# A two-layer decoder trunk on one core: q, k and z projected transposed, with high and low activations side by side

## The chip, the cores and the metric

The kernel runs on one core of a Trainium2 chip. The metric is the device time of one execution in microseconds (us). The program is written instruction by instruction for each engine: TensorE (PE in the profile; its weight loads are PEld), VectorE (DVE), ScalarE (ACT), GpSimd (POOL) and SyncE (SP, which issues DMAs). Semaphores alone order the engines against each other.

## The reference

The input is 256 tokens of width 2048 in fp32. Layer 0 is retention, layer 1 is sparse attention, each behind an RMS norm and with a SiLU gate. Cut to what matters here:

```python
h = x
hn = rmsnorm(h, norm_g[0])                      # layer 0: retention, 8 heads
q, k, v, gate = split(hn @ ret_w_in)            # per head 256, 256, 512, 512 columns
scores = einsum(q, k * dk**-0.5) * decay
o = groupnorm(scores @ v (+ state))             # per head and token, no gain
h = h + (silu(gate) * o) @ ret_w_out
hn = rmsnorm(h, norm_g[1])                      # layer 1: 16 heads in 4 groups
q, kc, vc, ks, vs, kw, vw, g, z = split(hn @ nsa_w_in)   # 2048, 6 x 512, 48, 2048 columns
k_cmp, v_cmp = mlp(blocks of kc), mlp(blocks of vc)
o = g0*attend(q, k_cmp, v_cmp) + g1*attend(q, ks, vs) + g2*attend(q, kw, vw)   # g = sigmoid
h = h + (silu(z) * o) @ nsa_w_out
out = rmsnorm(h, final_g)
```

## The kernel before

**Weights.** All weights come in chunks of 512 rows by 512 columns (four tiles of 128 rows, 1 MB), 200 in all, through a ring of four slots. SP loads a chunk into `w_raw` when VectorE is through with the chunk four places earlier. ScalarE rounds it to `w_hi` (L417) when TensorE is through with the chunk four places earlier, and VectorE takes the rest, `w_lo = w_raw - w_hi` (L639). Both run two chunks ahead of TensorE (`ahead`). The activations, transposed, are kept in two rounded parts as well, `hT_hi` and `hT_lo`.

**One chunk on TensorE** (`chunk`, L943 to L945). For each of two token tiles and each of four row tiles three products of 512 columns are made, 24 in all; the activations are the stationary operand and the weights stream:

```python
pe.matmul(o, xT_hi[:, k0 + i, tok], w_hi[:, s, i, :], start=a, stop=False)
pe.matmul(o, xT_hi[:, k0 + i, tok], w_lo[:, s, i, :], start=False, stop=False)
ins = pe.matmul(o, xT_lo[:, k0 + i, tok], w_hi[:, s, i, :], start=False, stop=z)
```

A projection of the norm's output takes four such chunks (2048 rows) and ends in a pair of PSUM banks, one for each token tile; an output chunk (`out_chunk`) is complete in itself. There are two pairs of banks in `acc` that take turns, and four `side` banks. A pair is given back as a whole, by `acc_free`.

**From tokens to transposed.** q and k of a head (one projection of 256 + 256 columns), kc, vc, ks, kw, a group's q and a group's z are all needed with features on partitions. VectorE (`take`, L672) or ScalarE (`take_z`, L577, with SiLU) scales the pair by rstd into `stage`, TensorE turns `stage` with eight transposes into `side[0:2]` (L980), and ScalarE and VectorE copy them to qT and kT (L476, L730), rawT, ksT, kwT (L545), qhT (L514) or silu_zT (L583).

**Order of work.** It is written out by hand, as chunks c with steps between them.

- *Retention, head h*: chunks 0 to 3 are q and k, 4 to 7 v, 8 to 11 the gate, 12 to 15 the output of head h - 1 (none for head 0). After chunk 4 the transposes, after chunk 5 the scores (L1016, L1018), after chunk 8 the weighted values (L1026 to L1028), after chunk 0 of the next head the transposes of y. Four more output chunks follow the last head, with the norm's transposes between them.
- *The k/v part*: seven projections (kc, vc, ks, vs, q of group 0, kw, vw), c = 0 to 27. Between them stand the compressions (L1107), the gates (48 products of 256 columns, L1132 to L1134) and the first scores. POOL computes rstd (L368).
- *Groups g = 0 to 3*: group 0 has 8 chunks (z, q of the next group), groups 1 and 2 have 12 (z, q, output of the group before), group 3 has 8 (z, output). The table `SLOTS` says behind which chunk a head's scores (L1081), the transposes of its probabilities (L1153) and the weighted values (L1166, between the two tiles of chunk 7 or 8) come. Each head's scores pass from TensorE to VectorE (add the distances, maximum; `head_scores`), to ScalarE (exponentials; `head_exps`) and to VectorE (`head_probs`, L802 to L810). In VectorE's program `head_probs` stands ahead of the low pass of its chunk (`ahead`), and reads of PSUM stand behind it. Four last output chunks follow group 3.

`add_residual` (L664) adds an output chunk's pair to the residual.

## Time and profile before

| | us |
|---|---|
| median of 3 runs (1268.44 to 1268.94) | 1268.67 |
| the profiled execution's own time | 1269.46 |
| its span, first to last instruction | 1267.7 |
| PE busy | 1244.6 (98%) |
| PEld busy | 1022.0 (81%) |
| DVE busy | 697.7 (55%) |
| ACT busy | 543.8 (43%) |
| POOL busy | 59.3 (5%) |

The span leaves 1.8 us of the profiled execution outside. The mean granted TensorE clock is 0.996 of full speed. The DMA engines moved 221.62 MB at a mean of 175 GB/s. The records of products overlap each other: a 512-column product is on record for 390 to 395 ns and the next one starts before it ends, so a product's cost is the distance from its start to the next start, not its duration. "Idle before" in a row is the time in which the engine had no record open, so a gap between starts is longer by what the last product would have taken anyway.

### The profile page before, as it was taken

The numbers are of one execution on the slowest core, as the hardware profiler recorded it, in microseconds if no ns is written. First come the engines' busy times: TensorE is split into PE (matmuls) and PEld (weight loads), VectorE is DVE, ScalarE is ACT, GpSimd is POOL, SyncE is SP. The second block draws the span as 40 slices with busy tenths as digits, with TensorE's granted clock in tenths as the row PEclk, the third lists the DMA queues.
The fourth block names the chain that finished last, engine by engine and source line by source line (L and its number), as shares of the span: only waits on it lengthen the run. The fifth ranks groups of instructions, "written<-read, shape, count | busy, mean of one in ns | idle before, by whom it ended". The sixth has DMA issues, their size and how long they took to land.

```text
span 1267.7 us, 15041 instructions
## 1 busy us (share of the span) xinstructions
PE 1244.6 (98%) x5734; PEld 1022.0 (81%) x5734; DVE 697.7 (55%) x768; ACT 543.8 (43%) x680; POOL 59.3 (5%) x53
## 2 busy tenths in 40 slices
PE   7999999999999999999999999999999999999997
PEld 6878888888888888888888888888878687887875
DVE  5545465364474564464465576444446475665765
ACT  6344243343342353343334354233346374472653
POOL 1010100100100100100100111000000000000000
PEclk9999999999999999999999999999999999999999
DMA  9635655556455465564564585646434234534432
GB/s 334 240 133 200 199 166 176 188 165 207 157 191 206 146 208 175 165 219 145 165 232 150 163 267 200 201 133 232 166 107 160 100 133 166 166 133 139 159 104 96
DMA packets 129304, 221.62 MB, mean 175 GB/s; under 512 B 6769, under 2 KB 39745, under 8 KB 129009
## 3 DMA queue, kind: packets, MB, share of 16 engines
q1 hardware_dynamic: 127360, 213.94, 50.6%
q0 software_dynamic: 1712, 7.07, 1.8%
q8 instruction: 26, 0.43, 0.1%
q14 instruction: 14, 0.11, 0.0%
q10 hardware_dynamic: 192, 0.08, 0.0%
HBM read 218.96 MB, written 2.10 MB: 174 GB/s over the span
## 4 chain that ended last, share of the span: by engine, by line
PE 98%; DVE 1%; DMA 0%; ACT 0%; issue 0%; POOL 0%; POOLq 0%; DVEq 0%; ACTq 0%
PE acc L943 28%; PE acc L945 28%; PE acc L944 28%; PE side L980 2%; PE side L1081 2%; PE side L1166 2%; PE side L1107 1%; PE side L944 1%; PE side L945 1%; PE side L943 1%; PE side L1153 1%; PE side L1168 1%; PE side L972 1%; PE side L1016 1%; PE side L1028 0%; PE side L1027 0%
## 5 line engine op out<-in xcount | busy, mean ns | idle before, releaser
L639 DVE TENSOR_TENSOR w_lo<-w_raw,w_hi 128x2048 fp32r<-128x2048 f32 x199 | 452.6, 2286 | 219.4 <-ACT w_hi L417 217.3
L943 PE MATMUL acc<-w_hi,hT_hi 128*128 128x512 f32 x1280 | 506.2, 395 | 3.3 <-DVE vw L672 1.5
L945 PE MATMUL acc<-w_hi,hT_lo 128*128 128x512 f32 x1280 | 499.5, 390 | 0.0
L944 PE MATMUL acc<-w_lo,hT_hi 128*128 128x512 f32 x1280 | 498.9, 390 | 0.0
L417 ACT CAST w_hi<-w_raw 128x2048 fp32r<-128x2048 f32 x199 | 374.4, 1909 | 116.0 <-PE acc L945 115.0
L943 PEld LDWEIGHTS acc<-w_hi,hT_hi 128*128 128x128 f32 x1280 | 240.9, 188 | 54.0 <-issue 3.4
L945 PEld LDWEIGHTS acc<-w_hi,hT_lo 128*128 128x128 f32 x1280 | 240.6, 188 | 50.8
L944 PEld LDWEIGHTS acc<-w_lo,hT_hi 128*128 128x128 f32 x1280 | 241.1, 188 | 48.9
L943 PE MATMUL acc<-w_hi,yT_hi 128*128 128x512 f32 x264 | 104.3, 395 | 0.0
L945 PE MATMUL acc<-w_hi,yT_lo 128*128 128x512 f32 x264 | 102.9, 390 | 0.0
L944 PE MATMUL acc<-w_lo,yT_hi 128*128 128x512 f32 x264 | 102.8, 389 | 0.0
L672 DVE TENSOR_SCALAR stage<-acc,rstd 128x512 f32<-128x512 f32 x32 | 22.5, 746 | 71.4 <-PE acc L945 71.4
L943 PEld LDWEIGHTS acc<-w_hi,yT_hi 128*128 128x128 f32 x264 | 49.6, 188 | 12.4 <-issue 2.3
L664 DVE TENSOR_TENSOR res<-acc,res 128x512 f32<-128x512 f32 x80 | 51.3, 683 | 12.6 <-PE acc L945 12.2
L945 PEld LDWEIGHTS acc<-w_hi,yT_lo 128*128 128x128 f32 x264 | 49.6, 188 | 10.5
L944 PEld LDWEIGHTS acc<-w_lo,yT_hi 128*128 128x128 f32 x264 | 49.6, 188 | 10.0
L526 ACT ACTIVATE arena<-arena,negmax 128x128 f32<-128x128 f32 x64 | 28.4, 445 | 58.4 <-DVE negmax L795 58.4
L372 POOL TENSOR_TENSOR head_rstd<-mv,eps 128x2 f32<-128x2 f32 x8 | 17.2, 2149 | 631.8 <-DVE mv L698 631.8
L487 ACT ACTIVATE silu_gate<-acc,rstd 128x512 f32<-128x512 f32 x16 | 10.1, 684 | 70.3 <-PE acc L945 70.3
L744 DVE SCALAR_TENSOR_TENSOR v_lo<-acc,rstd,v_hi 128x512 fp32r<-128x512 f32 x16 | 11.3, 747 | 48.5 <-ACT v_hi L483 48.5
L476 ACT COPY qT<-side 128x512 f32<-128x512 f32 x8 | 4.7, 587 | 76.7 <-PE side L980 76.7
L483 ACT ACTIVATE v_hi<-acc,rstd 128x512 fp32r<-128x512 f32 x16 | 10.1, 685 | 62.7 <-PE acc L945 62.7
(148 smaller groups left out, 792.0 us busy)
## 6 DMA issues: line engine op xcount, KB each, us to landing
w_raw<-in_ret_w_in SPq DMA_DIRECT2D x192, 512.0 KB, 4.6
w_raw<-in_nsa_w_in SPq DMA_DIRECT2D x112, 512.0 KB, 4.5
w_raw<-in_ret_w_out SPq DMA_DIRECT2D x64, 512.0 KB, 4.6
w_raw<-in_nsa_w_out SPq DMA_DIRECT2D x32, 512.0 KB, 4.9
res<-in_x SPq DMA_DIRECT2D x4, 512.0 KB, 8.9
arena<-in_nsa_cmp_w_k POOLq DMA_DIRECT2D x1, 2048.0 KB, 13.1
arena<-in_nsa_cmp_w_v POOLq DMA_DIRECT2D x1, 2048.0 KB, 12.0
out<-w_raw SPq DMA_DIRECT2D x4, 512.0 KB, 3.6
```

The costliest lines, as they stand in the source:

```text
L372: pool.tensor_tensor(head_rstd[:, :], mv[:, :, 1], eps[:, :], ALU.add).then_inc(head_rstd_step, 1)
L417: act.copy(w_hi[:, s, :, :], w_raw[:, s, :, :]).then_inc(hi_done, 1)
L526: act.activation(prob[:, b, a:z], prob[:, b, a:z], ACT.Exp, bias=negmax[:, t, b + 1:b + 2], accum_out=sums[:, t, b + 1:b + 2])
L639: dve.tensor_tensor(w_lo[:, s, :, :], w_raw[:, s, :, :], w_hi[:, s, :, :].bitcast(F32), ALU.subtract).then_inc(lo_done, 1)
L664: ins = dve.tensor_tensor(at, acc[pair][t][:, :], at, ALU.add)
L672: ins = dve.tensor_scalar(to[:, t, :], acc[pair][t][:, :], rstd[:, layer, t:t + 1], None, ALU.mult)
L943: pe.matmul(o, xT_hi[:, k0 + i, tok], w_hi[:, s, i, :], start=a, stop=False)
L944: pe.matmul(o, xT_hi[:, k0 + i, tok], w_lo[:, s, i, :], start=False, stop=False)
L945: ins = pe.matmul(o, xT_lo[:, k0 + i, tok], w_hi[:, s, i, :], start=False, stop=z)
L980: ins = pe.transpose(side[banks[i // 2]][:, at:at + P], src[:, t, i * P:(i + 1) * P], ident[:, :])
L1081: ins = pe.matmul(side[2 + b][:, a - extra:z], qhT[:, r, t * P:(t + 1) * P], keys[:, 0:z - a + extra], start=True, stop=True)
L1166: pe.matmul(side[2 + t][:, :], v_now[:, 2 * b + keys, :], pT[:, b, tile, :], start=first, stop=False)
```

## The change

**The product.** The 20 projections that are needed transposed are now made so (`chunk_T`). A slice m of 128 of the chunk's 512 weight columns is the stationary operand, and the activations stream: `hT` holds high and low side by side, [128, 16, 2, 256], so that one product of 512 columns makes w_hi x hi in the left half of a bank and w_hi x lo in the right half; a second one of 256 columns adds w_lo x hi to the left half. A chunk has 16 of each. The four slices of a projection are in the four banks `parts[0..3]`, which are the two banks of pair 0 and the two of pair 1. Every slice has a single bank.

**Reading it.** ScalarE copies a bank's right half to `low_part` (`take_low`; the fourth copy takes the room of the first, so it waits for VectorE's first add), and VectorE adds the left half to it, straight into qT and kT, rawT, ksT, kwT, qhT or silu_zT (`take_T`). The staging reads, the transposes and the copies behind them are gone. In layer 1 a pass of 128 x 1024 then multiplies by rstd along the free axis (`scale_T`), and z has its SiLU in place (`silu_z`, at c = 5). The row of rstd comes once from two small products behind chunk 2 of the k/v part. In layer 0 the keys' rstd goes into the decay pass; the queries' rstd is left out, since the group norm takes a token's factor out again, and its epsilon is multiplied by the token's mean square instead (`head_stats`).

**Banks.** `acc_free` is counted per bank, and TensorE waits for each bank (`bank_free`). v is now in pair 0 and the gate in pair 1; output chunks take pair j % 2, where before they took the order 1, 0, 1, side in the heads; vs and vw go to side[0:2]. The scores of a head come behind chunk 4 instead of 5. At the start VectorE copies the second set of columns ahead of a norm step instead of behind it.

The diff, cut to its core:

```diff
-            def take(chunk, pair, to, layer):
+            def take_v(chunk, to):
...
+            def take_T(at, *to):
+                for m in range(4):
+                    dve.wait_ge(low_copied, 4 * at + m + 1)
+                    dve.tensor_tensor(to[m], parts[m][:, 0:S], low_part[m % 3], ALU.add).then_inc(acc_free[m // 2], 1)
+            def scale_T(to, uses, scale=1.0):
+                row = bass.AP(rstd_row.tensor, rstd_row.offset, [rstd_row.ap[0], [0, 4], [1, S]])
+                for pair in range(2):
+                    dve.wait_ge(*bank_free(pair, 1, uses[pair]))
+                dve.scalar_tensor_tensor(out=to, in0=to, scalar=scale, in1=row, op0=ALU.mult, op1=ALU.mult).then_inc(scaled, 1)
...
+            def take_low(at, chunk, first_two):
+                for m in range(4):
+                    act.wait_ge(*((part_done, 3 * at + m + 1) if m < 3 else (chunk_done, chunk)))
+                    if m == 3:
+                        act.wait_ge(*bank_free(0, 0, first_two))
+                    act.copy(low_part[m % 3], parts[m][:, S:2 * S]).then_inc(low_copied, 1)
...
+            def silu_z(g):
+                act.wait_ge(scaled, z_at(g) - H + 1)
+                act.activation(silu_zT, silu_zT, ACT.Silu).then_inc(zT_ready, 1)
...
+            def chunk_T(q, c, uses, between=None):
+                s = c % RING
+                n = 4 * q + s
...
+                for m in range(4):
+                    if m == 2 and between:
+                        between()
+                    if s == 0 and not known(uses[0], 0):
+                        pe.wait_ge(*bank_free(m // 2, m % 2, uses[m // 2]))
...
+                    w = slice(m * P, (m + 1) * P)
+                    for i in range(KPC):
+                        k = KPC * s + i
...
+                        pe.matmul(parts[m][:, :], w_hi[:, s, i, w], hT[:, k, :, :], start=(k == 0), stop=False)
+                        ins = pe.matmul(parts[m][:, 0:S], w_lo[:, s, i, w], hT[:, k, 0, :], start=False, stop=(k == KT - 1))
+                    if s == RING - 1 and m < 3:
+                        ins.then_inc(part_done, 1)
+                ins.then_inc(chunk_done, 1)
...
                 for c, kind in enumerate(kinds):
                     ahead(q, c)
                     if c == 3:
-                        take_z(q)
+                        take_low(z_at(g), 4 * q + 4, nsa_uses(g)[0] + 1)
+                    if c == 7 and "q" in kinds:
+                        take_low(z_at(g) + 1, 4 * q + 8, nsa_uses(g)[0] + 2)
...
-                    if c == at["zT"]:
-                        take_zT(g)
-                    if c == at["qT"] and "q" in kinds:
-                        take_q(g + 1)
+                    if c == 5:
+                        silu_z(g)
...
+                    if c == 3:
+                        take_T(z_at(g), *(silu_zT[:, m, :] for m in range(4)))
+                    if c == 4:
+                        scale_T(silu_zT, (u0 + 1, u1 + 1))
                     if c == 7 and "q" in kinds:
-                        take(4 * q + 8, 0, stage, 1)
+                        take_T(z_at(g) + 1, *(qhT[:, m, :] for m in range(4)))
+                        scale_T(qhT, (u0 + 2, u1 + 2), float(DH) ** -0.5)
```

**The order on the engines, at three places.** TensorE in head 0, where the q/k projection ends and the v projection goes on. Before, at the end of chunk 4 (the transposes, then chunk 5):

```order
L943 MATMUL acc<-w_hi,hT_hi 128x512
L944 MATMUL acc<-w_lo,hT_hi 128x512
L945 MATMUL acc<-w_hi,hT_lo 128x512
L980 MATMUL side<-ident,stage 128x128 x8
L943 MATMUL acc<-w_hi,hT_hi 128x512
```

Now, from the last products of chunk 3 to the first of chunk 4:

```order
L989 MATMUL acc<-hT,w_hi 128x512
L990 MATMUL acc<-hT,w_lo 128x256
L989 MATMUL acc<-hT,w_hi 128x512
L990 MATMUL acc<-hT,w_lo 128x256
L959 MATMUL acc<-w_hi,hT 128x512
L960 MATMUL acc<-w_lo,hT 128x512
L961 MATMUL acc<-w_hi,hT 128x512
```

The transposes are gone from behind chunk 4, and the q/k chunks alternate a wide and a narrow product.

VectorE in group 0, from the end of `head_probs` at c = 3 on. Before (arena holds the probabilities):

```order
L810 TENSOR_SCALAR arena<-arena,factor 128x15 x2
L639 TENSOR_TENSOR w_lo<-w_raw,w_hi 128x2048 x2
L787 SCALAR_TENSOR_TENSOR arena<-dist,slopes,side 128x414
L789 SCALAR_TENSOR_TENSOR arena<-dist,slopes,side 128x128
L789 SCALAR_TENSOR_TENSOR arena<-dist,slopes,side 128x256
```

Now (L668 is `take_T`, L675 `scale_T`, L630 the low pass; stage holds the low parts and the row of rstd):

```order
L812 TENSOR_SCALAR arena<-arena,factor 128x15 x2
L630 TENSOR_TENSOR w_lo<-w_raw,w_hi 128x2048
L668 TENSOR_TENSOR arena<-acc,stage 128x256 x4
L630 TENSOR_TENSOR w_lo<-w_raw,w_hi 128x2048
L675 SCALAR_TENSOR_TENSOR arena<-arena,stage 128x1024
L789 SCALAR_TENSOR_TENSOR arena<-dist,slopes,side 128x414
```

The four reads of z's banks stand behind the probabilities and one low pass.

ScalarE in the loop of groups 1 and 2, from the last exponentials at c = 5 on. Before (L583 copies z's transposes):

```order
L529 ACTIVATE arena,sums<-arena,negmax 128x15 x2
L414 ISA
L416 ISA
L417 CAST w_hi<-w_raw 128x2048
L581 REGISTER_ALU
L583 COPY arena<-side 128x512 x2
L416 REGISTER_ALU
L417 CAST w_hi<-w_raw 128x2048
L570 COPY arena<-side 128x3x128
```

Now (L575 is `silu_z`, L465 `take_low`):

```order
L533 ACTIVATE arena,sums<-arena,negmax 128x15 x2
L574 REGISTER_ALU
L575 ACT_TABLE_LOAD
L575 ACTIVATE arena<-arena 128x1024
L414 ISA
L416 ISA
L417 CAST w_hi<-w_raw 128x2048
L416 REGISTER_ALU
L417 CAST w_hi<-w_raw 128x2048
L462 ISA
L465 COPY stage<-acc 128x256
```

The table load and the SiLU stand ahead of both casts, and the first copy of q's low half behind them.

## Rows read from the trace of the kernel before

**Rows 1.** The page's chain that ended last, shares of the span by engine:
```profile
PE 98%; DVE 1%; DMA 0%; ACT 0%; issue 0%; POOL 0%; POOLq 0%; DVEq 0%; ACTq 0%
```
**Rows 2.** Timeline of PE, head 3 (start us, us, engine, line, op, tiles, shapes):
```profile
302.08 0.39 PE L943 MATMUL acc<-w_hi,hT_hi 128*128 128x512 f32 x1
...
305.71 0.39 PE L944 MATMUL acc<-w_lo,hT_hi 128*128 128x512 f32 x1
```
**Rows 3.** Timeline of PE, the gates' 48 products:
```profile
916.74 0.28 PE L1133 MATMUL acc<-hT_lo,yT_hi 128*128 128x256 f32 x1
...
922.13 0.28 PE L1134 MATMUL acc<-hT_hi,yT_lo 128*128 128x256 f32 x1
```
**Rows 4.** Timeline of PE, the transposes of vc in the k/v part:
```profile
817.57 1.04 PE L980 MATMUL side<-ident,stage 128*128 128x128 f32 x8
818.36 0.47 PE L943 MATMUL acc<-w_hi,hT_hi 128*128 128x512 f32 x1
818.67 0.39 PE L944 MATMUL acc<-w_lo,hT_hi 128*128 128x512 f32 x1
```
**Rows 5.** Groups of instructions by form, weight loads of a projection:
```profile
L943 PEld LDWEIGHTS acc<-w_hi,hT_hi 128*128 128x128 f32 x1280 | 240.9, 188 | 54.0 <-issue 3.4 <-DVE vw L672 1.9
```
**Rows 6.** Timeline of PE, gaps behind head 0 and before z:
```profile
87.66 0.49 PE L943 MATMUL acc<-w_hi,hT_hi 128*128 128x512 f32 x1 [1.46 <-ACT silu_gate L487]
...
940.25 0.39 PE L945 MATMUL acc<-w_hi,hT_lo 128*128 128x512 f32 x1
942.14 0.50 PE L943 MATMUL acc<-w_hi,hT_hi 128*128 128x512 f32 x1 [1.50 <-DVE vw L672]
```
**Rows 7.** Timeline of PE, boundary of groups 0 and 1:
```profile
1001.91 0.39 PE L945 MATMUL acc<-w_hi,hT_lo 128*128 128x512 f32 x1
...
1006.12 1.72 PE L1081 MATMUL side<-ksT,arena 128*128 128x143 f32 x4 [1.22 <-issue]
...
1009.61 0.40 PE L945 MATMUL acc<-w_hi,hT_lo 128*128 128x512 f32 x1
```
**Rows 8.** Stretches: us, busy of PE PEld DVE ACT POOL, clock, DMA, GB/s:
```profile
1006.00:1007.00 1.00, 0.88 (x3) 0.91 (x4) 0.00 (x0) 0.02 (x1) 0.00 (x0) 0.50 0.00 0
1009.00:1010.00 1.00, 1.00 (x5) 0.81 (x4) 0.84 (x3) 0.00 (x0) 0.00 (x0) 0.79 0.00 0
```
**Rows 9.** Timeline of DVE, end of the first probabilities:
```profile
945.99 0.36 DVE L810 TENSOR_SCALAR arena<-arena,factor 128x15 f32<-128x15 f32 x2
```
**Rows 10.** Timeline of POOL, rstd of the second layer:
```profile
773.93 2.64 POOL L368 TENSOR_TENSOR rstd<-meansq,minus_half 128x2 f32<-128x2 f32 x1
```
**Rows 11.** Waits of DVE (us in total, times, longest us):
```profile
DVE stage L672 <- PE acc L945: 71.4, 14, 6.6
```
**Rows 12.** Timelines, group 0 at c = 3: end of chunk, cast, low pass:
```profile
968.37 0.39 PE L945 MATMUL acc<-w_hi,hT_lo 128*128 128x512 f32 x1
968.21 1.89 ACT L417 CAST w_hi<-w_raw 128x2048 fp32r<-128x2048 f32 x1
970.13 2.29 DVE L639 TENSOR_TENSOR w_lo<-w_raw,w_hi 128x2048 fp32r<-128x2048 f32 x1
```
**Rows 13.** Groups of instructions by form, durations:
```profile
L736 DVE TENSOR_TENSOR sT<-side,decays 128x256 f32<-128x256 f32 x8 | 3.4, 424 | 17.1 <-PE side L1018 17.1
L631 ACT ACTIVATE w_raw<-w_raw,rstd 128x1024 f32<-128x1024 f32 x2 | 2.3, 1150 | 2.3 <-POOL rstd L368 2.3
L577 ACT ACT_TABLE_LOAD x4 | 5.1, 1283 | 0.1
```
**Rows 14.** Timelines, group 1: cast after the last exponentials, start of c = 8:
```profile
1053.82 1.89 ACT L417 CAST w_hi<-w_raw 128x2048 fp32r<-128x2048 f32 x1
1061.26 0.47 PE L943 MATMUL acc<-w_hi,yT_hi 128*128 128x512 f32 x1
```
**Rows 15.** Timelines, end of group 1: last product, last add:
```profile
1092.90 0.39 PE L945 MATMUL acc<-w_hi,yT_lo 128*128 128x512 f32 x1
1096.97 1.28 DVE L664 TENSOR_TENSOR res<-acc,res 128x512 f32<-128x512 f32 x2
```

More of the change, by code:

```diff
@@ L95, in trunk @@
         stage = sb("stage", [P, TT, COLS])
+        stage_row = stage[:, :, :].rearrange("p t n -> p (t n)")
+        rstd_row = stage_row[:, 3 * S:4 * S]
+        low_part = [stage_row[:, i * S:(i + 1) * S] for i in range(3)]
         ksT = sb("ksT", [P, G, NC + S])
@@ L180, in trunk @@
         acc = pair_banks + [side[0:2]]
+        parts = [pair_banks[m // 2][m % 2] for m in range(4)]
         raw_in = [sem(f"raw_in{s}") for s in range(RING)]
@@ L473, in retention @@
                         squares(0, 2 + c)
-                    if c == 4:
-                        act.wait_ge(qkT_psum, h + 1)
-                        act.copy(qT[:, :, :], side[0][:, :].rearrange("p (a b) -> p a b", a=2)).then_inc(qT_ready, 1)
+                    if c == 3:
+                        if first:
+                            act.wait_ge(squares_done, CG)
+                        take_low(h, n0 + 4, ret_uses(h) + 1)
                     if c == 6:
@@ L822, in _ @@
                 if c in (3, 7, 11, 19, 23):
-                    take(n, (c // 4 + 1) % 2, stage, 1)
+                    if c == 3:
+                        dve.wait_ge(rstd_row_ready, 1)
+                    if c == 7:
+                        dve.wait_ge(window_ready, 1)
+                    if c == 19:
+                        dve.wait_ge(hid_psum, 2)
+                    i = KV_T[c // 4]
+                    to = (rawT, rawT, ksT[:, :, NC:NC + S], qhT, kwT[:, :, :])[i]
+                    take_T(H + i, *(to[:, m, :] for m in range(4)))
+                    scale_T(to, (KV_USES + i + 1, KV_USES + i + 1), float(DH) ** -0.5 if c == 19 else 1.0)
                 if c in (4, 8):
@@ L924, in _, with chunk @@
         def _(pe):
-            def chunk(q, s, xT_hi, xT_lo, k0, pair, start, stop, tile_ready=None, between=None, tile0_done=None):
+            def chunk(q, s, xT_hi, xT_lo, k0, banks, start, stop, free=None, tile_ready=None, between=None, tile0_done=None):
                 n = 4 * q + s
-                by_halves = known(n, 0)
-                pe.wait_ge(*((first_lo, 1) if by_halves else (lo_done, n + 1)))
+                pe.wait_ge(lo_done, n + 1)
                 for t in range(TT):
@@ L934, in chunk @@
                         between()
+                    if free:
+                        pe.wait_ge(*free(t))
                     if tile_ready:
@@ L1003, in retention @@
                     if c == 4:
-                        pe.wait_ge(acc_free[0], u0 + 1)
-                        if not first:
-                            pe.wait_ge(side_read, side_reads(h))
-                        transpose_tiles(stage, (0, 1)).then_inc(qkT_psum, 1)
-                    if c == 5:
-                        pe.wait_ge(qT_ready, h + 1)
-                        pe.wait_ge(kT_ready, h + 1)
+                        for pair in range(2):
+                            pe.wait_ge(*bank_free(pair, 1, u + 1))
                         if not first:
```

245 lines of the change are left out of this document (104 added, 141 removed).

## The prediction

> **What bounds the kernel now.** I read the chain of waits first [rows 1]: TensorE is 98% of it, so only TensorE's time and its gaps count. Next, how far apart its products start, since their records overlap. In [rows 2] sixteen 512-column products take 305.71 - 302.08 = 3.63 us, 0.227 us each; a chunk of 24 takes 5.45. In [rows 3] 47 products of 256 columns, on rounded values as those of the projections are, take 922.13 - 916.74 = 5.39 us, 0.115 us each. A block of eight transposes stands in [rows 4]: 0.79 us until the next product starts, and that one takes 0.31 instead of 0.23, so a block costs 0.87. Last, the gaps: two of about 1.5 us [rows 6], and one group boundary that takes 7.70 us from 1001.91 to 1009.61, with two waits [rows 7] and half the clock behind them [rows 8].
>
> **Removed.** 20 blocks of transposes go (one per transposed projection: 8 heads, 5 in the k/v part, 4 z, 3 q). 19 of them stand in a full stream: 19 x 0.87 = **-16.6 us**. The twentieth is in [rows 7]. There TensorE waits for VectorE, transposes, waits for ScalarE's copies, and starts the scores at 1006.12, at half clock. Now the low copy and the last add end about 0.9 us behind the chunk (0.42 each [rows 13]), VectorE's combine having ended within the chunk's second half; then comes the scaling pass of 1024 columns, half of the 2048-column pass of 2.29 us in [rows 12], so 1.2, and with two hand-overs the scores start 2.3 us behind the chunk. From the start of the scores to 1009.61 pass 3.49 us, of which the clock costs 1.7 (below). At full clock the stretch takes 0.2 + 2.3 + 1.8 = 4.3 instead of 7.70: **-3.4**.
>
> In [rows 6] the first gap is a wait for the SiLU read of the pair that the next chunk wants. Now the gate is in pair 1 and the next head starts in pair 0: **-1.6** (1.46 and the slower first product). The second is z waiting for the read of vw, which moves to side banks: 1.6 less. But VectorE finishes the first probabilities at 946.35 [rows 9], and z's first chunk would now end at 940.25 + 0.23 + 5.46 = 945.94, so TensorE waits 0.4 at the transposes behind it: **-1.2**. Gains: 16.6 + 3.4 + 1.6 + 1.2 = 22.8.
>
> **Added on TensorE.** A transposed chunk has 16 products of 512 and 16 of 256 columns: 16 x (0.227 + 0.115) = 5.47 against 5.45, and 80 such chunks (20 projections of four) give **+1.6**. No row shows the two widths in turn. Below, nothing excludes 0.107 for the small one (256 columns at 2.4 GHz), which is -10 us in all; above, a weight load takes 0.188 from start to end [rows 5], and if each small product had to wait for its own, that would be 16 x (0.188 - 0.115) x 80 = +94. I take the row of the same width and rounded type. The row of rstd costs two more products like a transpose, some 0.3 with the change of type, and needs POOL's rstd, done at 776.57 [rows 10], just when chunk 2 ends: **+0.4**.
>
> The Trainium skill ("TensorE: Matmul & The Clock Gate", Back-to-back issue gap) speaks against the change: it gives 81 ns for 128-column and 131 ns for 512-column products in a real stream, so a large fixed part for each. By an estimate from that page 256 columns cost 98 ns and a chunk goes from 24 x 131 to 16 x (131 + 98) ns, +0.52 us, +42 in all. The trace disagrees with it: 227 ns and 115 ns, nearly in proportion.
>
> **Waits that the four banks bring.** Before, a pair had four chunks until it was needed again. Now the next chunk takes slice 0's bank at once, so VectorE's add must be done by the end of the chunk. In the heads and the k/v part it is: VectorE waited for TensorE at 14 of the 16 reads into stage [rows 11] (the two others are those at c = 7 of groups 1 and 2), and slice 0 is complete three quarters of a chunk early. ScalarE now waits in take_low until the chunk ends, so its next cast comes 5 us later, but that weight is needed two chunks (10.9 us) later, and 0.5 + 1.9 + 2.3 us are enough; the transfer behind it has six chunks. In the sparse part it isn't so:
>
> - *Groups 0 and 3, c = 4.* In front of take_T stand head_probs and a low pass. In group 0 ScalarE casts at 968.21, VectorE's low pass starts at 970.13 [rows 12] and the next would follow 2.2 us later, at 972.4; with an add of 0.42 [rows 13] the bank is free at 972.8. TensorE's chunk ends at 968.37 + 0.23 = 968.6. Gap 4.2 us; group 3 has the same order of work: **+8.4**. Before, the next chunk took the other pair, so nobody waited.
> - *Groups 1 and 2, c = 8.* silu_z stands between ScalarE's exponentials and two casts: a table load of 1.28 and a pass of 1024 columns, 1.15 [rows 13], where two copies of 1.05 stood between the casts. From 1053.82 [rows 14] the casts end at 1053.8 + 2.4 + 3.7 = 1060.0. VectorE's two low passes follow the first cast (1058.2) and end at 1062.6, the add at 1063.0. TensorE, without the z block, is there at 1061.26 - 0.87 = 1060.4. Gap 2.7, twice: **+5.4**.
> - *End of groups 1 and 2.* The last out chunk ends at 1092.90 + 0.23; slice 2 of the next z comes half a chunk later, at 1095.9, and wants the bank that VectorE's add from 1096.97 reads until 1097.7 [rows 15]. Before, q wanted it four chunks later. Gap 1.8, twice: **+3.7**.
>
> At c = 4 of groups 1 and 2 transposed probabilities and scores (2 us of TensorE) cover the add with under 1 us to spare; I count nothing.
>
> Without the clock: -22.8 + 1.6 + 0.4 + 8.4 + 5.4 + 3.7 = **-3.3 us**.
>
> **The clock.** Behind the waits of 1.5 us the products run at full rate [rows 6]. From 1002.1 to 1006.1 TensorE did nothing but eight transposes, and the granted clock fell to 0.50, 1.2 GHz, until 1009.4 (the slice of 0.79 was low for 0.4 us) [rows 8]: 3.4 us at half rate, which cost 1.7. A gap of 4.2 us with nothing in it is as long, so I let the clock fall at both: **+3.4**. For the gaps of 2.7, 2.3 and 1.8 the rows on either side (1.5 and 4.0) bound it: nothing, or 1.7 for each; 2.7 is about in the middle, the others nearer to 1.5, and nothing is taken.
>
> **Sum:** -3.3 + 3.4 = +0.1 against the profiled execution's 1269.46 us. That one is 0.8 us above the median of 1268.67, which I take as the base: **1268.8 us**. A measurement of this kernel can tell about 0.2%, 2.5 us, from no change.
>
> **The rivals.**
> - *The clock doesn't fall in the gaps.* For: full rate after 1.5 us. Against: [rows 8]. Then 1268.7 - 3.3 = 1265.4, faster.
> - *The clock falls at the gaps of 2.7 us too* (slower than before): bank waits at c = 8 of groups 1 and 2 that grow into lost clock. It decides whether 2.7 us of waiting is enough. +3.4: 1272.2; with the three gaps of about 2 us as well 1277. The Trainium skill ("TensorE: Matmul & The Clock Gate", HAM oscillation) says that waits of some microseconds inside a loop can let the clock drop each time, and that the cost is then paid at every one; this trace shows one such case and two against it.
> - *A small product doesn't overlap its load behind a wide one.* For: every second load has only 0.115 us beside it. Against: 48 in a row did so [rows 3]. Already 32 ns per small product would cost 41 us: 1310, and the full bound gives 1363. The skill's figures above would also give 1310.
> - *The gaps at c = 4 aren't there*, the change doesn't wait as I read it: no 8.4 and no fall of the clock: 1257.0.
>
> **How the numbers follow.** My case 0.47 (its own range 1266.5 to 1271.5), no fall of the clock 0.20, falls at 2.7 us too 0.18, no gaps at c = 4 0.09, small products slow 0.06. Faster by over 0.2%: 0.20 + 0.09 + 0.01 of my own case = 0.30; slower: 0.18 + 0.06 + 0.02 = 0.26; the same: 0.44. The range leaves out the last two cases and the far end of the second rival, under 0.2 together: 1263.5 to 1275.0.
>
> **What would show it.** TensorE's two lines of a transposed chunk alternate at 0.227 and 0.115 us; no transposes of stage are left; before the fifth chunk of groups 0 and 3 TensorE is idle for about 4.2 us, released by VectorE's add, and for 2.7 us at c = 8 of groups 1 and 2; the granted clock is 0.50 twice for about 3.4 us. I am wrong if a transposed chunk takes over 5.6 us, if heads show gaps at c = 4, or if the clock falls more or less often.

## The result and the profile after

The changed kernel takes 1280.79 us (median of 4 runs, 1280.21 to 1282.06), the kernel before 1268.81 us on the same chip (4 runs, 1268.44 to 1269.42): ratio 1.0095, 95% interval 1.0078 to 1.0113. It is 12.0 us slower. The forecast was 1268.8 with a range of 1263.5 to 1275.0, so the measured time lies above the range. In the profiled executions the spans (first to last instruction) are 1278.8 and 1267.7 us: 11.1 us to explain.

The page of the changed kernel (busy time of each engine; the chain that ended last; two groups of part 5), which answers to [rows 1]:

```profile
PE 1243.3 (97%) x6218; PEld 1040.4 (81%) x6218; DVE 717.7 (56%) x820; ACT 552.9 (43%) x724; POOL 59.3 (5%) x53
...
PE 92%; DVE 3%; ACT 2%; issue 2%; DMA 0%; DVEq 0%; POOL 0%; POOLq 0%; ACTq 0%
...
L989 PE MATMUL acc<-hT,w_hi 128*128 128x512 f32 x1280 | 457.3, 401 | 7.4 <-DVE arena L668 4.1
...
L990 PE MATMUL acc<-hT,w_lo 128*128 128x256 f32 x1280 | 358.5, 280 | 0.0
```

Before, TensorE was 98% of the chain; now VectorE, ScalarE and "issue" (time in which the engine waited for nothing that the profile shows) have 7% of it between them. A glance at the busy time misleads: it fell by only 1.3 us (1244.6 to 1243.3), though the transposes are gone. So TensorE lost time in two ways, by waiting and by doing the new products more slowly than costed.

**The waits.** The waits of TensorE (us in total, times, longest us):

```profile
PE acc L959 <- DVE arena L668: 8.5, 3, 4.1
...
PE acc L989 <- DVE arena L668: 4.1, 1, 4.1
PE acc L989 <- DVE res L655: 3.2, 2, 1.6
PE side L1107 <- issue: 2.3, 1, 2.3
```

And where they stand, in the timeline of PE: c = 4 of group 0, end of group 0, c = 8 of group 1, end of group 1, c = 8 of group 2, end of group 2, c = 4 of group 3. They answer to [rows 6, 7, 14, 15]:

```profile
965.86 0.77 PE L989 MATMUL acc<-hT,w_hi 128*128 128x512 f32 x1 [4.06 <-DVE arena L668]
...
1003.88 0.48 PE L1107 MATMUL side<-ksT,arena 128*128 128x143 f32 x2 [2.30 <-issue]
...
1061.24 0.50 PE L959 MATMUL acc<-w_hi,yT_hi 128*128 128x512 f32 x1 [2.21 <-DVE arena L668]
...
1096.78 0.50 PE L989 MATMUL acc<-hT,w_hi 128*128 128x512 f32 x1 [1.61 <-DVE res L655]
...
1148.45 0.64 PE L959 MATMUL acc<-w_hi,yT_hi 128*128 128x512 f32 x1 [2.22 <-DVE arena L668]
...
1185.60 0.49 PE L989 MATMUL acc<-hT,w_hi 128*128 128x512 f32 x1 [1.60 <-DVE res L655]
...
1213.81 0.77 PE L959 MATMUL acc<-w_hi,yT_hi 128*128 128x512 f32 x1 [4.06 <-DVE arena L668]
```

All seven are where the forecast put them, with forecast lengths of 4.2, 2.3, 2.7, 1.8, 2.7, 1.8 and 4.2. Without the one of 2.30, whose place was already slow before, they are 15.8 us of idle time. By the starts of the products, which is how the forecast counted, each gap is 0.16 us longer (the last record before it outlasts its product's share), 16.8 us in all. Neither gap of [rows 6] is left.

**The clock.** The stretches at half clock (us, busy time of PE, PEld, DVE, ACT, POOL, granted clock, DMA share, GB/s), which answer to [rows 8]:

```profile
964.30:971.10 6.80, 5.24 (x16) 4.49 (x17) 5.50 (x7) 2.17 (x2) 0.00 (x0) 0.50 0.47 154
1005.30:1008.70 3.40, 3.40 (x12) 2.89 (x11) 2.46 (x7) 0.59 (x3) 0.00 (x0) 0.50 0.00 0
...
1148.70:1152.10 3.40, 3.40 (x9) 2.62 (x9) 2.34 (x5) 3.40 (x7) 0.00 (x0) 0.50 1.03 382
1213.50:1216.90 3.40, 3.09 (x7) 2.48 (x8) 2.10 (x5) 2.17 (x2) 0.00 (x0) 0.50 0.60 170
```

If half of what TensorE worked in them is lost, that is (5.24 + 3.40 + 3.40 + 3.09) / 2 = 7.6 us. The rows of the first stretch say a little less:

```profile
961.52 0.28 PE L990 MATMUL acc<-hT,w_lo 128*128 128x256 f32 x1
...
966.64 0.63 PE L989 MATMUL acc<-hT,w_hi 128*128 128x512 f32 x1
...
967.28 0.63 PE L989 MATMUL acc<-hT,w_hi 128*128 128x512 f32 x1
```

A pair (the products that follow each other in a transposed chunk, see below) takes 0.64 us at half clock and 0.349 at full, so 46% is lost and not 50% (768 columns at 1.2 GHz are 0.64 us with nothing on top); by that the four stretches cost 7.0 us. Before there was one such stretch among the products, of 3.4 us. The gap of 2.21 us before 1061.24 left the clock at 1.00; the one of 2.22 us before 1148.45, the same place one group later, did not.

**The products.** The timeline of PE in head 1, two pieces: the transposed chunk 0, and chunk 1 behind the transposes of the gate. [Rows 2] are what the 512-column products did before:

```profile
85.56 0.28 PE L990 MATMUL acc<-hT,w_lo 128*128 128x256 f32 x1
...
90.86 0.28 PE L990 MATMUL acc<-hT,w_lo 128*128 128x256 f32 x1
90.98 1.04 PE L1018 MATMUL side<-ident,silu_gate 128*128 128x128 f32 x8
...
92.43 0.28 PE L990 MATMUL acc<-hT,w_lo 128*128 128x256 f32 x1
...
97.64 0.27 PE L990 MATMUL acc<-hT,w_lo 128*128 128x256 f32 x1
```

Between the first two rows lie 15 pairs (a product of 512 and one of 256 columns): 5.30 / 15 = 0.353 us. Between the last two lie 15 as well: 5.21 / 15 = 0.347. Single pairs take between 340 and 361 ns, in a pattern that repeats every two or three pairs; the mean over a stretch, outside gaps and half clock, is 346.7 or 353.3 ns but for the first pair or two, and a whole stretch keeps to one of them. 71% of the pairs are in stretches of the first kind, and the mean is 348.6. The forecast had 342. So 1280 pairs took 1280 x 0.3486 = 446.2 us, and the 1920 products of 512 columns that they replace 1920 x 0.2271 = 436.0: **+10.2 us**, where the ledger had +1.6.

With that the ledger comes to the 11.1 us: gains as forecast, -16.6 - 3.4 - 1.6 - 1.2 = -22.8; products +10.2 and row of rstd +0.4; gaps +15.8; clock +7.6. Sum +11.2. That it meets the spans to 0.1 is partly luck: with the gaps by their starts (16.8) and the clock by the pairs' rows (7.0) it is 11.6, so it closes to about half a microsecond. (The medians differ by 12.0 because the profiled execution of the kernel before was 0.6 us above its median and that of the changed kernel 0.2 below.)

The largest of the gains can be read by itself. Behind chunk 0 of a head TensorE transposes the y of the head before, in both kernels. In heads 1 and 7, before, and in head 7, now (head 1 is the row at 90.98 above):

```profile
93.23 1.03 PE L980 MATMUL side<-ident,silu_gate 128*128 128x128 f32 x8
...
647.07 1.04 PE L980 MATMUL side<-ident,silu_gate 128*128 128x128 f32 x8
```

```profile
642.58 1.04 PE L1018 MATMUL side<-ident,silu_gate 128*128 128x128 f32 x8
```

The changed kernel is 2.25 us ahead at the first and 4.49 at the second, 0.37 for each of six heads. Its 64 pairs a head (16 in the slower kind of stretch, 48 in the faster) take 22.28 us against 21.80 for 96 products of 512 columns, so the block of transposes that is gone was worth 0.37 + 0.48 = 0.85 us, where the forecast had 0.87.

What was open was why a pair costs what it does, whether gaps and clock account for the rest, and whether the transposed form is worth having without them.

### The profile page after: what moved, and what is told of

It is laid out like the page before. It is cut to its first block, busy times and chain, and to the rows that moved or that the text cites. A ratio compares the mean times of both kernels' runs of the same rounds, so it can differ in the third digit from the quotient of the medians.

```text
span 1278.8 us, 16211 instructions
## 1 busy us (share of the span) xinstructions
PE 1243.3 (97%) x6218; PEld 1040.4 (81%) x6218; DVE 717.7 (56%) x820; ACT 552.9 (43%) x724; POOL 59.3 (5%) x53
## 4 chain that ended last, share of the span: by engine, by line
PE 92%; DVE 3%; ACT 2%; issue 2%; DMA 0%; DVEq 0%; POOL 0%; POOLq 0%; ACTq 0%
PE acc L989 21%; PE acc L959 16%; PE acc L961 16%; PE acc L960 16%; PE acc L990 11%; PE side L1107 2%; PE side L1188 2%; PE side L959 1%; PE side L961 1%; PE side L960 1%; PE side L1131 1%; PE side L1175 1%; PE side L1190 1%; ACT arena L530 1%; ACT w_hi L417 1%
## 5 line engine op out<-in xcount | busy, mean ns | idle before, releaser
L630 DVE TENSOR_TENSOR w_lo<-w_raw,w_hi 128x2048 fp32r<-128x2048 f32 x199 | 452.2, 2288 | 237.9 <-ACT w_hi L417 235.0
L989 PE MATMUL acc<-hT,w_hi 128*128 128x512 f32 x1280 | 457.3, 401 | 7.4 <-DVE arena L668 4.1
L990 PE MATMUL acc<-hT,w_lo 128*128 128x256 f32 x1280 | 358.5, 280 | 0.0
L989 PEld LDWEIGHTS acc<-hT,w_hi 128*128 128x128 f32 x1280 | 242.7, 190 | 65.7 <-DVE w_lo L630 4.4
L990 PEld LDWEIGHTS acc<-hT,w_lo 128*128 128x128 f32 x1280 | 243.4, 190 | 0.8
L959 PE MATMUL acc<-w_hi,hT 128*128 128x512 f32 x576 | 225.1, 391 | 0.0
L961 PE MATMUL acc<-w_hi,hT 128*128 128x512 f32 x576 | 224.4, 390 | 0.0
L960 PE MATMUL acc<-w_lo,hT 128*128 128x512 f32 x576 | 224.2, 389 | 0.0
L959 PE MATMUL acc<-w_hi,yT_hi 128*128 128x512 f32 x320 | 127.3, 398 | 8.5 <-DVE arena L668 8.5
L961 PEld LDWEIGHTS acc<-w_hi,hT 128*128 128x128 f32 x576 | 108.1, 188 | 22.8
L959 PEld LDWEIGHTS acc<-w_hi,hT 128*128 128x128 f32 x576 | 108.2, 188 | 22.2
L960 PEld LDWEIGHTS acc<-w_lo,hT 128*128 128x128 f32 x576 | 108.2, 188 | 22.1
L465 ACT COPY stage<-acc 128x256 f32<-128x256 f32 x80 | 28.5, 370 | 108.4 <-PE acc L990 96.5
```

What stands on the lines that cost most here:

```text
L465: act.copy(low_part[m % 3], parts[m][:, S:2 * S]).then_inc(low_copied, 1)
L630: dve.tensor_tensor(w_lo[:, s, :, :], w_raw[:, s, :, :], w_hi[:, s, :, :].bitcast(F32), ALU.subtract).then_inc(lo_done, 1)
L989: pe.matmul(parts[m][:, :], w_hi[:, s, i, w], hT[:, k, :, :], start=(k == 0), stop=False)
L990: ins = pe.matmul(parts[m][:, 0:S], w_lo[:, s, i, w], hT[:, k, 0, :], start=False, stop=(k == KT - 1))
```

## Experiments

"Before" is the same kernel on every chip; it took 1269.28 (7 runs), 1269.53 (19) and 1269.37 us (6) beside the three batches below. Times of experiments are medians of 4 to 10 runs, and ratios are to before.

### Products of one width together

```diff
@@ chunk_T @@
                         pe.matmul(parts[m][:, :], w_hi[:, s, i, w], hT[:, k, :, :], start=(k == 0), stop=False)
+                    for i in range(KPC):
+                        k = KPC * s + i
                         ins = pe.matmul(parts[m][:, 0:S], w_lo[:, s, i, w], hT[:, k, 0, :], start=False, stop=(k == KT - 1))
```

> The changed kernel, but each slice of a transposed chunk makes its four 512-column products first and its four 256-column products behind them, instead of in turn. Theory A (a product costs more where the width changes): 8 changes a chunk instead of 32, so three quarters of the 10.3 us that the transposed chunks cost over their forecast go, and the time is about 1273 us, a transposed chunk about 5.48 us. Theory B (every product whose stationary operand is a slice of a weight chunk costs about 4 ns more, whatever stands next to it): nothing moves, 1281 us, chunk 5.55 to 5.65.

Measured: 1283.45 us, ratio 1.0115 (1.0098 to 1.0132). The timeline of PE, in which four products of a width now stand in one row (the last row is cut off by the end of the window):

```profile
94.66 1.08 PE L989 MATMUL acc<-hT,w_hi 128*128 128x512 f32 x4
...
96.06 1.09 PE L989 MATMUL acc<-hT,w_hi 128*128 128x512 f32 x4
...
97.46 0.87 PE L989 MATMUL acc<-hT,w_hi 128*128 128x512 f32 x3
```

Four pairs take 1.40 us, 0.350 each, with a quarter of the changes of width. If each change of width cost something, the time would have come down; it went up by 2.7 us (2.2 when each is taken against its own "before"). The theory of the width change (A) falls. Mixing the widths is not free for all that: in this trace a 512-column product behind another one of its width starts 232.9 ns after it in the mean, where in a stream of that width alone ("Everything wide", below) it is 227.1.

### Everything narrow

```diff
@@ chunk_T @@
-                        pe.matmul(parts[m][:, :], w_hi[:, s, i, w], hT[:, k, :, :], start=(k == 0), stop=False)
+                        if k == 0:
+                            pe.matmul(parts[m][:, :], w_hi[:, s, i, w], hT[:, k, :, :], start=True, stop=False)
+                        else:
+                            pe.matmul(parts[m][:, 0:S], w_hi[:, s, i, w], hT[:, k, 0, :], start=False, stop=False)
+                            pe.matmul(parts[m][:, S:2 * S], w_hi[:, s, i, w], hT[:, k, 1, :], start=False, stop=False)
```

> The changed kernel, but the 512-column product is split into two of 256 columns (high half, low half), except in the first of the sixteen row tiles, so that chunks 1 to 3 of a projection consist of 48 narrow products in a row. Theory A: 48 x 0.1147 = 5.51 us a chunk, about 0.1 less than now, and about 1276 us. Theory B: 48 x 0.117 = 5.62 or more, no faster than the changed kernel (1281 us or more).

Measured: 1292.8 us, ratio 1.0187 (1.0170 to 1.0204). The timeline of PE in head 1:

```profile
93.86 0.28 PE L992 MATMUL acc<-hT,w_hi 128*128 128x256 f32 x1
...
97.94 0.28 PE L993 MATMUL acc<-hT,w_hi 128*128 128x256 f32 x1
```

Here 34 intervals take 4.08 us: 0.120 for a product of 256 columns with nothing but its like around it. Not 0.115. With 0.227 for 512 columns the line through both is 107 ns for 256 columns (which is 256 columns at 2.4 GHz, clock 1.00) and **13 ns for the product itself**, of either width. A pair is then 227 + 120 = 347, as in the faster of its two kinds.

### Everything wide

The low weights multiply both halves. This adds the product of low weights and low activations, which the algorithm leaves out, to the result.

```diff
@@ chunk_T @@
-                        ins = pe.matmul(parts[m][:, 0:S], w_lo[:, s, i, w], hT[:, k, 0, :], start=False, stop=(k == KT - 1))
+                        ins = pe.matmul(parts[m][:, :], w_lo[:, s, i, w], hT[:, k, :, :], start=False, stop=(k == KT - 1))
```

> The changed kernel, but the low weights multiply both halves too, so all 32 products of a transposed chunk have 512 columns (the low x low part is added to the result). Theory A: 32 x 0.227 = 7.26 us a chunk, about 1280.8 + 80 x 1.68 = 1415 us. Theory B: 32 x 0.231 to 0.233 = 7.4 to 7.46, 1426 to 1431 us.

Measured: 1401.58 us, ratio 1.105 (1.1029 to 1.1072), below what both theories gave. The timeline of PE:

```profile
100.36 0.39 PE L990 MATMUL acc<-hT,w_lo 128*128 128x512 f32 x1
...
103.77 0.39 PE L989 MATMUL acc<-hT,w_hi 128*128 128x512 f32 x1
```

15 intervals, 3.41 us: 0.227 each, the same as in the token form. So a stationary slice of a weight chunk costs nothing extra, and theory B falls too. So of the extra time in a pair the 13 ns are there in streams of one width too, and only the step from 347 to 353 is found in mixed streams alone. The total fits: 1280 x (454.2 - 348.6) ns = +135.2; a slower TensorE waits less, 6.3 us instead of 15.8 at the same places (two waits of 2.3 and 2.4, two of 0.8), and the clock falls once instead of four times (-5.9): +119.8, where the spans differ by 119.1.

### A token product in two halves

This asks whether the 13 ns belong to the transposed form.

```diff
@@ chunk (token form) @@
-                        ins = pe.matmul(o, xT_lo[:, k0 + i, tok], w_hi[:, s, i, :], start=False, stop=z)
+                        pe.matmul(o[:, 0:S], xT_lo[:, k0 + i, tok], w_hi[:, s, i, 0:S], start=False, stop=False)
+                        ins = pe.matmul(o[:, S:2 * S], xT_lo[:, k0 + i, tok], w_hi[:, s, i, S:2 * S], start=False, stop=z)
```

> The changed kernel with each third product of the token chunks (high weights by low activations, 512 columns of weights moving, activations stationary; 960 of them) made as two of 256 columns. Transposed chunks are untouched. Theory F (every product costs its columns at 2.4 GHz and a fixed 13.4 ns, whatever its width and whatever is stationary): the pair costs 240 ns in place of 227, +12.9 us: about 1293.5. Rival T (the extra belongs to the transposed form, with weights stationary; in the token form a narrow product costs what the 46 intervals of the gates' row give, 117.2 ns): 234, +7 us: 1287.5. Rival A (the cost is in each change of width, some 9 ns per pair of changes as between the pair's 349.9 and 227.1 + 113.6): over 1297.

Measured: 1293.59 us, ratio 1.0189 (1.0169 to 1.0208); theory F had 1293.5, a nearer match than its terms deserve, as the rows show. The activations are stationary here, and one more product in each group of three costs as much as in the transposed form. By the starts a group of four takes 697 ns against 3 x 227.1 = 681 for three, +16; 960 times that is 15 us, of which 13 ns each are the fourth product, and the rest is of the size of the step from 347 to 353. The pairs of the transposed chunks, which the edit doesn't touch, took 347.8 instead of 348.6 ns in the mean (-1.0 us). The spans differ by 13.9.

### Narrower still

```diff
@@ chunk_T, on the reordered kernel below @@
-                        ins = pe.matmul(parts[m][:, 0:S], w_lo[:, s, i, w], hT[:, k, 0, :], start=False, stop=(k == KT - 1))
+                        pe.matmul(parts[m][:, 0:P], w_lo[:, s, i, w], hT[:, k, 0, 0:P], start=False, stop=False)
+                        ins = pe.matmul(parts[m][:, P:S], w_lo[:, s, i, w], hT[:, k, 0, P:S], start=False, stop=(k == KT - 1))
```

> The reordered kernel (1259.8 us) with each product of 256 columns in the transposed chunks made as two of 128 columns (1280 more products). Theory F (columns at 2.4 GHz and a fixed 13.4 ns for each product): a product of 128 columns takes 53.3 + 13.4 = 66.7 ns, the pair 133.5 in place of 120, +17.2 us: about 1277. Rival L (a product can't come faster than the loads of its stationary matrix: those take 188 ns from start to end, and at 120 ns spacing two of them already overlap): at a floor of 120 ns for each, 240 for the pair, +154 us: over 1400; any spacing over 80 ns speaks for a floor of that kind. Which also bounds the rival of the prediction in which small products wait for their loads.

Measured: 1395.39 us, ratio 1.0988 (1.0969 to 1.1008). Theory F fails at this width. The timeline of PE:

```profile
94.10 0.45 PE L999 MATMUL acc<-hT,w_hi 128*128 128x512 f32 x1
94.39 0.22 PE L1000 MATMUL acc<-hT,w_lo 128*128 128x128 f32 x1
94.45 0.28 PE L1001 MATMUL acc<-hT,w_lo 128*128 128x128 f32 x1
94.56 0.45 PE L999 MATMUL acc<-hT,w_hi 128*128 128x512 f32 x1
```

The three take 0.457 us from start to start. Without the 0.227 of the wide one, 0.230 is left for the two of 128 columns: 0.115 each, nearly what a product of 256 takes. Half the columns save almost nothing; 1280 times the 0.107 that the second one adds is 137 us, and the time rose by 135.6. The floor that rival L expected, 0.120, was the right size. The rows say more than the mean does: the two short products start only 0.06 us apart (94.39 and 94.45), 0.29 behind the wide one and 0.11 ahead of the next. So a short product can follow another much faster than 0.115, and the floor isn't in the rate of the products. The loads of the stationary matrices in the same stretch, timeline of PEld:

```profile
94.05 0.19 PEld L999 LDWEIGHTS acc<-hT,w_hi 128*128 128x128 f32 x1
94.16 0.19 PEld L1000 LDWEIGHTS acc<-hT,w_lo 128*128 128x128 f32 x1
94.39 0.19 PEld L1001 LDWEIGHTS acc<-hT,w_lo 128*128 128x128 f32 x1
94.50 0.19 PEld L999 LDWEIGHTS acc<-hT,w_hi 128*128 128x128 f32 x1
```

They start 0.11, 0.23 and 0.11 us apart, and of the 7497 distances between loads in this trace 28 are below 107 ns. That points to the loads, which come no more often than every 0.11 us or so, as what a product of 128 columns waits for; no edit here tests it by itself.

### The waits taken out by order alone

In the groups of 8 chunks, at c = 3, the low part's copies and adds go ahead of the casts and of the probabilities; the SiLU goes one chunk before the values; the last add of a group of 12 goes ahead of the low passes. Nothing is computed differently.

```diff
@@ ScalarE, sparse(g) @@
-                    ahead(q, c)
+                    early = c == 3 and len(kinds) == 8
+                    if not early:
+                        ahead(q, c)
                     if c == 3:
                         take_low(z_at(g), 4 * q + 4, nsa_uses(g)[0] + 1)
+                    if early:
+                        ahead(q, c)
...
-                    if c == 5:
+                    if c == at["values"] - 1:
                         silu_z(g)
@@ VectorE, sparse(g) @@
+                    early = c == 3 and len(kinds) == 8
+                    if early:
+                        take_T(z_at(g), *(silu_zT[:, m, :] for m in range(4)))
                     if c in at["factors"]:
...
+                    add_first = kind == "out" and c == at["next_factors"]
+                    if add_first:
+                        add_residual(4 * q + c, c % 2, c % 4)
                     ahead(q, c)
...
```

> The changed kernel with another order on VectorE and ScalarE in the sparse part: reads of z's banks at c = 3 of groups 0 and 3 ahead of the probabilities and of the weight passes, z's SiLU behind the last copies of probabilities instead of at c = 5, the last add of an out chunk ahead of its low pass. If the six bank waits (4.1, 2.2, 1.6 us, twice each, 15.8 in all) and the falls of the clock behind them (four of five low stretches, 6.8 us) are what my ledger says: 1258 to 1262 us, gaps at these places under 0.6 us. Rival: the weight passes that are now later become the wait, and the time stays above 1270 us.

Measured: **1259.82 us**, ratio 0.993 (0.9913 to 0.9946): 21.0 us below the changed kernel, 9.5 below before. The waits of TensorE, all that are left but those for the input at the start:

```profile
PE side L1117 <- issue: 2.3, 1, 2.3
PE acc L999 <- DVE w_lo L688: 0.4, 1, 0.4
PE acc L999 <- DVE arena L672: 0.3, 1, 0.3
PE acc L969 <- DVE arena L672: 0.3, 1, 0.3
```

The wait of 0.4 is in the first projection; 0.7 us is left at the places of the edit. The clock is 1.00 until the last microseconds of the profiled execution. The gaps (15.8, less 0.7) and the clock (7.6) are 22.7; the spans differ by 21.3, and from head 1 on this execution was already 1.05 us late, before any edit acts. That leaves 0.3 us. So gaps and clock together are confirmed to about that; the two runs below take them in parts.

Two parts of it alone. With the move at c = 3 only (a subset of the diff above):

> The changed kernel with one of the three moves of the reordered one: in the groups of 8 chunks ScalarE takes the low part before its casts and VectorE before the probabilities, at c = 3. The two gaps of 4.06 us at c = 4 of groups 0 and 3 go (8.1), with the low clock behind them (6.8 and 3.4 us, 5.1 lost): 1280.8 - 13.2 = 1267.6. That is if each fall of the clock belongs to its own gap. Rival (a fall at a gap of about 2.2 us hangs on what went before): the falls at the end of group 0 and at c = 8 of group 2 may go as well, 1.7 each: down to 1264.2.

Measured: 1270.66 us (10 runs, 1268.69 to 1271.43), ratio 1.0011 (1.0001 to 1.0020), so 10.1 us saved and not 13.2; both waits of 4.06 us are gone and the profiled span is 1267.9. The clock fell at the gaps of c = 8 in groups 1 and 2 and not at the end of group 0. In the changed kernel it fell at the end of group 0 and in group 2, but not in group 1, at gaps of the same length. So neither expectation holds: the smaller falls are not tied to their gaps, and they don't go with the large ones. One profiled execution a kernel shows one outcome of several, for the mean granted clock of the ten executions runs from 0.994 to 0.997, and below, with the same number of executions, from 0.991 to 0.995. With the other two moves only:

> The changed kernel with the two other moves of the reordered one: silu_z one chunk later and the last add before the casts. The gaps of 2.2 us at c = 8 of groups 1 and 2 and of 1.6 us at the end of groups 1 and 2 go (7.6), with one fall of the clock (1.7): 1280.8 - 9.3 = 1271.5. The gaps of 4.06 us at c = 4 of groups 0 and 3 stay, with their low clock (6.8 and 3.4 us). If the moves only help together with the third, which would mean that the gaps hide one another: little below 1280.

Measured: 1270.77 us (10 runs, 1267.58 to 1272.40), ratio 1.0009 (0.9999 to 1.0018). The time is near the 1271.5 of the expectation. The waits of 4 us stay; of the five smaller ones only that at the end of group 0 is left, so the gaps don't hide one another. In the profiled execution the clock fell for 3.4 us three times, and the first gap of 4 us, followed by 6.8 us of half clock in the changed kernel, had 3.4 behind it here. From 1280.8 the two parts save 10.1 and 10.0, together 20.1; the whole saves 21.0. They add up to within 1 us.

### What sets the 347 or 353

```diff
@@ chunk_T, on the reordered kernel @@
                         pe.wait_ge(*bank_free(m // 2, m % 2, uses[m // 2]))
+                        if m == 0:
+                            pe.transpose(parts[0][:, 0:P], ident[:, :], ident[:, :])
```

> On top of the reordered kernel (1259.8 us), TensorE makes one fp32 transpose of the identity into the bank that the first transposed chunk of a projection is about to open, before that chunk's first product; nothing else changes. In the traces so far a pair of products (512 columns, then 256) takes either 346.8 ns or 353 to 357 ns, the same value for a whole stretch, and the short value stands behind blocks of fp32 products, the long one behind plain projection chunks. Theory C (the state of a stretch is set by what TensorE did just before it, and an fp32 product resets it): all stretches come to 346.8 ns, which is worth about 3.7 us by the stretches of the reordered kernel (8 heads 1.3, the 256-product run of the k/v part 0.9, the rest 1.5); the 20 transposes cost about 0.13 each, 2.6: about 1258.7. Rival (the state has to do with which data are read, not with what came before): the long stretches stay, 1262.4.

Measured: 1261.15 us, ratio 0.9933 (0.9917 to 0.9950). The timeline of PE, chunk 0 of head 1 and chunk 1 of head 4:

```profile
90.24 0.27 PE L1002 MATMUL acc<-hT,w_lo 128*128 128x256 f32 x1
...
91.28 0.28 PE L1002 MATMUL acc<-hT,w_lo 128*128 128x256 f32 x1
...
368.77 0.28 PE L1002 MATMUL acc<-hT,w_lo 128*128 128x256 f32 x1
...
374.07 0.28 PE L1002 MATMUL acc<-hT,w_lo 128*128 128x256 f32 x1
```

Chunk 0 did come to 0.347 (1.04 / 3) here, as in six of the seven heads behind the first, but in head 4 chunk 1, behind a block of fp32 transposes as always, went to 5.30 / 15 = 0.353, and so it did in five of the seven. In all, 45% of the pairs are now of the slower kind, against 37% in the reordered kernel. An fp32 product doesn't set the faster kind: theory C falls. Nor is it the data: the same chunk of the same head is of one kind in one kernel and of the other in the next. Something at the start of a stretch decides, and what it is stays open. (The 357 ns of the expectation is a miscount: those stretches hold one wide product more than narrow ones. There are two kinds, not three.)

### A version that beats both

The wait of 2.30 us at the end of group 0 is the last slice's copy and add and a scaling pass over all four slices, but the first scores read slice 0 only. Slices 0 to 2 are scaled as soon as they are added, and TensorE waits for slice 3 before the scores that read it.

```diff
@@ VectorE, in place of take_T and scale_T for q @@
+            def take_q(g, uses):
+                at = z_at(g) + 1
+                for part in (range(3), range(3, 4)):
+                    for m in part:
+                        dve.wait_ge(low_copied, 4 * at + m + 1)
+                        dve.tensor_tensor(qhT[:, m, :], parts[m][:, 0:S], low_part[m % 3], ALU.add).then_inc(acc_free[m // 2], 1)
...
+                    dve.scalar_tensor_tensor(out=to, in0=to, scalar=float(DH) ** -0.5, in1=row, op0=ALU.mult, op1=ALU.mult).then_inc(scaled if n == 3 else scaled_last, 1)
...
@@ TensorE, head_scores @@
+                if r == 3 and not known(g, 0):
+                    pe.wait_ge(scaled_last, g)
```

> The reordered kernel (1259.8 us) with q's scaling pass in the groups split: slices 0 to 2 are scaled when they are added, slice 3 by itself behind its own add, and TensorE waits for the last slice only before the scores that read it. In the trace of the reordered kernel TensorE waits 2.30 us at the end of group 0, of which the last slice's low copy, add and a scaling pass of 1.22 us are the length. By the theory of the bank and queue waits the scores start about 1.8 us earlier, the gap is 0.5 or less, the clock stays: 1258.0. If the gap stands for something else (the release of the score banks): 1259.8.

Measured: **1256.40 us** (4 runs, 1256.06 to 1256.44), ratio 0.9898 (0.9880 to 0.9916), 13.0 us below before and 3.4 below the reordered kernel. VectorE and TensorE at the end of group 0:

```profile
995.09 0.96 DVE L695 SCALAR_TENSOR_TENSOR arena<-arena,stage 128x768 f32<-128x768 f32 x1
995.97 0.42 DVE L686 TENSOR_TENSOR arena<-acc,stage 128x256 f32<-128x256 f32 x1
996.42 0.42 DVE L695 SCALAR_TENSOR_TENSOR arena<-arena,stage 128x256 f32<-128x256 f32 x1
```

```profile
996.15 0.94 PE L1134 MATMUL side<-ksT,arena 128*128 128x143 f32 x4 [0.63 <-issue]
```

The gap is 0.63 instead of 2.30 and the scores run beside slice 3's scaling. That is 1.7 of the 2.9 us between the two spans. Another 1.0 stands at the start, where the edit does nothing: head 1 begins at 85.4 us here and began at 86.4 in the profiled execution of the reordered kernel. By the edit alone the gain is thus nearer to 1.7 than to 3.4.

## Why the prediction was wrong

By its own steps, in its order:

- *Removed transposes (-16.6; 19 x 0.87 is 16.5), boundary (-3.4), head 0 (-1.6), z (-1.2)*: right. No transposes of stage are left, both gaps of [rows 6] are gone, and TensorE is idle for 2.30 us before the scores of group 1, as forecast. Only the clock fell there after all. The block of transposes comes to 0.85 us against the forecast's 0.87 by the heads' own rows. No run undid the other parts singly; the evidence for them is the ledger, which closes to about 0.5 us.
- ***"A transposed chunk has 16 products of 512 and 16 of 256 columns: 16 x (0.227 + 0.115)", +1.6: this is the step that failed***, by 8.6 us (the 80 chunks cost 10.2 more than before, not 1.6). Three errors lie in it (together 8.2 us; the rest is rounding). First a miscount: [rows 3] name the second and the last of 48 products, so 5.39 us are 46 intervals and not 47, 0.117 and not 0.115 (+2.8 us over 1280 products). Then the row itself: in the gates' stream a small product takes 0.117, in these streams 0.120 (+3). Last the second kind of pair, 353 ns in 29% of cases (+2.4), which nothing in the trace before could show, since it had no such stream; why there are two kinds stays open. A check was at hand: the two widths give 227 = 213 + 14, so the small one could be expected at 107 + 14. I had looked at 0.107 as a lower bound and not asked what stood between it and the row. In the rival "a small product doesn't overlap its load" 32 ns per product were weighed; the truth was 7, small enough to be called nothing and multiplied by 1280.
- *Gaps at c = 4 (+8.4)*: right, 4.06 idle, 4.2 by the starts. VectorE's adds stood behind the probabilities and a low pass, as worked out. *At c = 8 (+5.4)*: 2.21 and 2.22 idle, 2.4 by the starts, instead of 2.7. *End of groups 1 and 2 (+3.7)*: 1.61 and 1.60 idle, 1.8 by the starts, as forecast. Together 16.8 us by the starts instead of 17.5.
- *"So I let the clock fall at both" and "nothing is taken" for the shorter gaps, +3.4*: **the second step that failed.** It cost 7.0 to 7.6. The first gap of 4.06 brought 6.8 us of half clock, not 3.4, and two gaps of 2.2 to 2.3 brought a fall each. The rival "falls at the gaps of 2.7 us too" named this, with 1272.2 to 1277; even it, with +1.6 for the products, fell short of the 1280.8 measured.
- *The rival from the skill*: the Trainium skill ("TensorE: Matmul & The Clock Gate", Back-to-back issue gap) speaks against the change, since by its figures each product has a large fixed part. The sign was right and I dropped it for the size: by an estimate from that page's figures a chunk would be 0.52 us longer, the runs show 0.13 (16 x 348.6 ns against 24 x 227.1). Its 131 ns for 512 columns stands against 227 measured here.

The range reached 6.2 us above the forecast. The clock's miss of about 4 us would have stayed within it; the products' 8.6 alone goes beyond it.

## What to carry to other kernels

When an edit changes how many products carry the same columns, cost each product as its columns plus a fixed part that you get from a row of the same trace (here 13 ns, which holds for 512 and 256 columns and no longer for 128), and count the intervals between rows, not the rows: 3 ns times a thousand products decides a case like this one. When a result bank is taken again at once, list what stands in front of the instruction that frees it on each queue; here the waits this made, 15.8 us and some 7 us of lost clock, went away by order alone, in three moves, and the same change then won 9.5 us in place of losing 12, and 13.0 with one scaling pass split as well. And price gaps of about 2 us and more with a share of lost clock behind them, not with nothing.

## What the runs showed of the hardware

- **The clock behind a gap.** In the profiled executions of the ten kernels that had such gaps, each of the 10 gaps of 3.9 to 4.1 us (idle time) was followed by half clock, or half clock began within it, seven times for 3.4 us and three times for 6.8. Of 22 gaps of 1.8 to 2.4 us 13 were followed by 3.4 us of it, with no order in it by length or place: the gap of 2.3 us at the end of group 0 was followed by a fall in six of ten kernels. Of the single gaps of 1.7 us or less none was, though before the change two of 1.50 and 1.22 us with only eight transposes between them were [rows 7, 8].
- **A fixed part.** A product of rounded fp32 operands takes 227 ns at 512 columns, whichever operand is stationary, and 120 at 256. Two of 128 columns behind a wide one take 230 together, though they start only 59 ns apart; the loads of stationary matrices stand 107 ns or more apart almost throughout.
- **Two kinds of stretch.** A stream of alternating 512- and 256-column products runs at a mean of 346.7 or 353.3 ns per pair and keeps to it until it is interrupted. A stream of 512 columns alone shows nothing of the sort, 227 throughout.
